# Rounds of 56 instead of 64 token slots per expert in a two-layer mixture-of-experts trunk on one core

## The chip, the core and the metric

The kernel runs on one core of one Trainium2 chip. The metric is the device time of one launch in microseconds (us); less is better. The engines named below are PE (TensorE: matmuls; its weight loads are listed apart as PEld), DVE (VectorE), ACT (ScalarE), POOL (GpSimd) and SP (SyncE, which here only issues DMAs).

## What is computed

Two layers over 256 tokens of 1024 features. Each layer is a mixer (three token mixers, gates, an output projection), a LayerNorm, then a shared expert plus 64 routed experts, then a LayerNorm. The change is in the routed experts:

```python
D_MODEL = 1024; SEQ = 256; DEPTH = 2
N_EXPERTS = 64; TOP_K = 8; N_GROUPS = 8; TOPK_GROUPS = 4; EXPERT_DIM = 256
...
def route(x_flat, router_w, router_bias):
    scores = jax.nn.sigmoid((x_flat @ router_w).astype(jnp.float32))
    choice = scores + router_bias.astype(jnp.float32)
    ...                                   # the best 4 of 8 groups, then the best 8 experts in them
    w = jnp.take_along_axis(scores, idx, axis=-1)
    w = w / jnp.sum(w, axis=-1, keepdims=True) * ROUTED_SCALE
...
    def one_block(args):                  # t: the tokens of a block, g: their gates, ex: its expert
        t, g, ex = args
        h = x_pad[t] @ w_gate_up[ex]
        h = jax.nn.silu(h[:, :EXPERT_DIM]) * h[:, EXPERT_DIM:]
        return (h @ w_down[ex]) * g[:, None]
```

Every token goes to 8 of 64 experts, so an expert gets 32 of the 256 tokens on average. On the inputs of the reference the fullest expert has 47 tokens in layer 0 and 51 in layer 1 (counted from its routing). All weights are float32; those of the experts are 3.1 MB each (1024 x 512 and 256 x 1024), 403 MB over both layers.

## The kernel before

**Slots.** Tokens are grouped by expert into slots. An expert has SLOTS = 64 slots in a round; an expert with more than 64 tokens would need a second round over all experts, and ROUNDS = 4 is the most there can be. `ranks` (L904) computes each token's rank in each of its experts (`slot_of`) and the largest count (`count_f`). `later_rounds` (L933) writes count - 1 as an integer to `count_i` (L936) and three further copies of `slot_of`, less 64, 128 and 192 (L938). `more_rounds` (L364) loads that integer on PE, ACT, DVE and SP and shifts it right by 6: the number of rounds beyond the first.

**Pairs.** Experts are worked two at a time, one pair per `pair_step`: 32 pair steps in a layer and round, 64 in all. The even and the odd pair step of a step number m share one gather for four experts. The pieces on PE, in the order in which PE issues them:

- L1393, "turn": two matmuls of 132 moving columns that turn the one-hot matrix and pick out the gates.
- L1406, up product: for each of 8 slices of 128 features and each of the 2 experts one matmul, 64 token columns held as weights, 512 columns of expert weights moving. Expert 0 writes partitions 0 to 63 of `bank_up`, expert 1 partitions 64 to 127, so the two use different column halves of the array. The trace has two records for each matmul of plain float32.
- L1361, gather (`gather`, L1349): fetches the tokens of four experts as columns. For each of 8 feature slices k, 4 matmuls (2 token halves t, and x split into `xg_hi` and `xg_lo`), each with 128 weight columns of x and 4 x 64 = 256 moving columns of `onehot`. All are float32r, one record each. It comes in quarters q = 0 to 3 of 8 matmuls, placed in the odd pair step only: q0 after the up product, q1 after the transposes, q2 after combine(1), q3 after the down product. Each quarter fills `bank_gather`, which ACT copies to `xe_t` (L696) before the next quarter may start.
- L1378, `combine`: 4 matmuls of 512 columns per half, float32r, for the pair step before.
- L1418: two transposes of `hid`.
- L1432, down product: built like the up product.

ACT applies silu (L707), DVE multiplies gate and up part (L1126), copies `hid_t` (L1129) and `onehot_t` (L1133), and both split the down product into `y_hi` (L713) and `y_lo` (L1140). The one-hot matrix of the next four experts is one DVE comparison of ranks with `iota` (`slots`, L942 to L947), 64 columns for each expert.

**Weights.** SP issues the loads of expert weights (`load_up` L478, `load_down` L482) in a fixed order. Three buffers take the pairs in turn up to pair 25 of a layer, two buffers the last six; a load waits until the up product (L488) or the down product (L492) of the pair before it in that buffer is done. After the last pair of layer 0 SP goes on to the projection weights of layer 1 (L469), whose split on ACT (L594) stands ahead of the last pair's silu.

**Order.** Every engine's program is written out by hand with semaphores; the pair steps are loops of six and of two steps. The lines around the gather:

```python
for c in range(2):
    k = 2 * q + c
    for t in range(TT):
        for part in (xg_hi, xg_lo):
            ins = mm(bank_gather[:, 2 * P * c:2 * P * c + 2 * P], part[:, t, k, :], onehot[:, t, :], ...)
```

Of the kernel before, what the change touches and what calls it, by code (L numbers as in the profile page):

```python
# [26 lines left out]
ALU = mybir.AluOpType  # L27
ACT = mybir.ActivationFunctionType
AX = mybir.AxisListType.X

P = 128
D = 1024
KD = D // P
S = 256
# [5 lines left out]
NE = 64  # L40
# [1 line left out]
FE = 256  # L42
KF = FE // P
SLOTS = 64
ROUNDS = S // SLOTS
GROUPS = 8
TOPK_GROUPS = 4
ROUTED_SCALE = 2.5
# [10 lines left out]
CONST = {}  # L59
CONST_COLS = 0  # L60
for _name, _width in (("ident", P), ("cos", S), ("sin", S), ("rotate", P), ("mask", S), ("iota", SLOTS),
                      ("earlier", GROUPS * GROUPS), ("ones", P), ("ramp", 4 * 16), ("before", P)):
    CONST[_name] = (CONST_COLS, CONST_COLS + _width)
    CONST_COLS += _width

# [71 lines left out]
def build(nc, x, w_in, rel_bias, pool_w, pool_scale, lambda_q1, lambda_k1, lambda_q2, lambda_k2, subln_g,  # L137
# [3 lines left out]
    with ExitStack() as ctx:  # L141
        def sb(name, shape, dt=F32):
            return ctx.enter_context(nc.sbuf_tensor(name, shape, dt))
# [29 lines left out]
        group_r = sb("group_r", [P, TT, GROUPS])  # L173
        wsum = sb("wsum", [P, TT])
        count_f = sb("count_f", [P, 1])
        count_i = sb("count_i", [P, L], I32)


        slot_of = sb("slot_of", [P, TT, ROUNDS * NE])
# [3 lines left out]
        onehot = sb("onehot", [P, TT, 2 * P], F32R)  # L183
# [38 lines left out]
        def view(at, *shape, dt=F32):  # L222
            size = 1
            for n in shape:
                size *= n
            words = size if dt == F32 else size // 2
            v = arena[:, at:at + words]
            if dt != F32:
                v = v.bitcast(dt)
            if len(shape) == 2:  # L230
                v = v.rearrange("p (a b) -> p a b", a=shape[0])
            elif len(shape) == 3:
                v = v.rearrange("p (a b c) -> p a b c", a=shape[0], b=shape[1])
            return v
# [2 lines left out]
        dn_b = view(8192, 2, KF, D)  # L237
        xg_hi, xg_lo = [nc.alloc_sbuf_tensor_at(name, [P, TT, KD, P], F32R, offset=arena_at + 4 * at)
                        for name, at in (("xg_hi", 12288), ("xg_lo", 14336))]
        xe_t = view(16384, KD, 2 * P)  # L240

        y_hi = nc.alloc_sbuf_tensor_at("y_hi", [P, D], F32R, offset=arena_at + 4 * 18432)
        y_lo = nc.alloc_sbuf_tensor_at("y_lo", [P, D], F32R, offset=arena_at + 4 * 19456)
# [26 lines left out]
        bank_gather, bank_even, bank_odd, bank_t = banks[4:8]  # L270
# [46 lines left out]
        count_ready = sem("count_ready")  # L317
# [9 lines left out]
        xe_ready = sem("xe_ready")  # L327
# [36 lines left out]
        def more_rounds(eng, l):  # L364

            eng.wait_ge(count_ready, l + 1)
            most = eng.value_load(count_i[0:1, l:l + 1], min_val=0, max_val=S - 1)
            return eng.snap(most >> 6).with_bounds(min_val=0, max_val=ROUNDS - 1)

        def x_tile(t, j):  # L370

# [213 lines left out]
        def _(act):  # L585
# [11 lines left out]
            for l in range(L):  # L597
                for task in PLAN:
# [19 lines left out]
                    elif kind == "z":  # L618
# [3 lines left out]
                        if name in ("ga", "gb", "gc"):  # L622

                            v = (i - 14) % 4
# [5 lines left out]
                        else:  # L630
                            dst = {"qa": qa_t, "ka": ka_t, "qc": qc_t, "kc": kc_t, "ub": ub_t}[name]
                            ins = nc.scalar.copy(dst[:, 2 * half:2 * half + 2, :], two)
# [60 lines left out]
                def gather_out(m, q):  # L693

                    act.wait_ge(gathered, 4 * m + q + 1)
                    nc.scalar.copy(xe_t[:, 2 * q:2 * q + 2, :],  # L696
                                   bank_gather[:].rearrange("p (c n) -> p c n", c=2)).then_inc(xe_ready, 1)

                def pair_step(n, odd, following=None, last=False):

# [40 lines left out]
        def _(dve):  # L741
            steps = [0]

            def step(ins):

                ins.then_inc(dve_step, 1)
                steps[0] += 1
# [185 lines left out]
            def later_rounds(l):  # L933

                wait_evac(dve, l, ("rank", 0, 0))
                v.tensor_scalar(count_i[:, l:l + 1], count_f[:], -1.0, None, ALU.add).then_inc(count_ready, 1)  # L936
                for r in range(1, ROUNDS):
                    step(v.tensor_scalar(slot_of[:, :, r * NE:(r + 1) * NE], slot_of[:, :, 0:NE], float(-SLOTS * r), None,  # L938
                                         ALU.add))
                settle()  # L940

# [220 lines left out]
        def _(pe):  # L1162
# [33 lines left out]
            for l in range(L):  # L1196
# [153 lines left out]
                def gather(m, q):  # L1350

                    if q == 0:
                        pe.wait_ge(s_ready, m + 1)
                    if q:

                        pe.wait_ge(xe_ready, 4 * m + q)
                    for c in range(2):
                        k = 2 * q + c
                        for t in range(TT):
                            for part in (xg_hi, xg_lo):  # L1360
                                ins = mm(bank_gather[:, 2 * P * c:2 * P * c + 2 * P], part[:, t, k, :], onehot[:, t, :],  # L1361
                                         start=(t == 0 and part is xg_hi), stop=(t == TT - 1 and part is xg_lo))
                    ins.then_inc(gathered, 1)

# [19 lines left out]
                def pair_step(n, m, first, odd, slot, loads, last=False):  # L1384
# [16 lines left out]
                    for k in range(KD):  # L1401
                        if not odd and k % 2 == 0:

                            pe.wait_ge(xe_ready, 4 * m + k // 2 + 1)
                        for e in range(2):
                            ins = mm(bank_up[SLOTS * e:SLOTS * e + SLOTS, :],  # L1406
                                     xe_t[:, k, P * odd + SLOTS * e:P * odd + SLOTS * e + SLOTS],
                                     gu[slot][:, e, k, :], start=(k == 0), stop=(k == KD - 1))
                    ins.then_inc(up_done, 1)
                    if odd and not last:  # L1410
# [64 lines left out]
def _constants():  # L1475
# [5 lines left out]
    def put(name, value):  # L1481
        a, b = CONST[name]
        c[:, a:b] = value
# [17 lines left out]
    mask = np.zeros((P, S), np.float32)  # L1501
    mask[:CHUNK, S - CHUNK:] = NEG
    put("mask", mask)
    put("iota", np.arange(SLOTS, dtype=np.float32)[None, :])
    g = np.arange(GROUPS)
    put("earlier", (g[None, :] < g[:, None]).astype(np.float32).reshape(1, -1))
    put("before", (p[:, None] < p[None, :]).astype(np.float32))
# [31 lines left out]
```

## Time and profile before

| | |
|---|---|
| time, median of 3 runs | 1582.39 us (1580.69 to 1586.14) |
| profiled execution, its own time | 1581.64 us |
| span from first to last instruction in it | 1579.8 us |
| PE busy | 1525.8 us, 97% of the span |
| DVE busy | 565.5 us, 36% |
| ACT busy | 414.4 us, 26% |
| moved by DMA | 495.86 MB, mean 314 GB/s |
| mean granted PE clock | 0.989 of full speed |

1.8 us of the profiled execution's time lie outside the span. An expert stage is the stretch of one layer in which L1406 and L1432 run: about 294 to 780 us and 1079 to 1564 us. The mixer stages lie before each. A PE that is listed as busy is not always computing: the records of matmuls overlap (one of the gather lasts 0.28 us and the next begins 0.12 us after it), so the distance from start to start says more than a record's length.

### The profile page before, as it was taken

How to read it: one execution, taken by the hardware profiler on the slowest of the kernel's cores; microseconds unless marked ns; L12 is line 12 of the kernel's file. 1: busy time of each engine (PE TensorE's matmuls, PEld its weight loads, DVE VectorE, ACT ScalarE, POOL GpSimd, SP SyncE). 2: the span in 40 equal slices, each digit the busy share in tenths (PEclk: the TensorE clock that was granted, in tenths of full speed). 3: DMA queues.
4: the chain of work that ended last, by engine and by line, in shares of the span. 5: the costliest groups of instructions: out<-in, count | busy, mean ns of one | idle time of the engine just before them, and what ended most of it. 6: DMA issues, size and time to landing. Idle time of an engine off the chain costs nothing.

```text
span 1579.8 us, 21900 instructions
## 1 busy us (share of the span) xinstructions
PE 1525.8 (97%) x8898; PEld 948.7 (60%) x8898; DVE 565.5 (36%) x1009; ACT 414.4 (26%) x655; POOL 34.5 (2%) x30
## 2 busy tenths in 40 slices
PE   7999999999999999999789999999999999999996
PEld 7899996444454444445388999864444444544542
DVE  4567735222222222222545577351222222212224
ACT  4545422121111112112235544221111211211111
POOL 0101000000000000000001110000000000000000
PEclk9999999999999999999989999999999999999998
DMA  8543458799999999699733544587999999996991
GB/s 292 175 170 138 153 206 374 288 426 424 415 421 414 405 417 414 244 414 419 282 107 107 187 161 160 210 331 317 426 425 416 419 401 416 419 411 249 415 412 75
DMA packets 79741, 495.86 MB, mean 314 GB/s; under 512 B 6080, under 2 KB 11456, under 8 KB 46656
## 3 DMA queue, kind: packets, MB, share of 16 engines
q1 hardware_dynamic: 77392, 491.31, 76.9%
q10 hardware_dynamic: 2288, 3.67, 0.7%
q8 instruction: 47, 0.77, 0.2%
q14 instruction: 14, 0.11, 0.0%
HBM read 493.92 MB, written 1.05 MB: 313 GB/s over the span
## 4 chain that ended last, share of the span: by engine, by line
PE 94%; DVE 2%; DMA 2%; ACT 1%; issue 1%; SPq 0%; DVEq 0%
PE bank L1406 28%; PE bank L1252 19%; PE bank L1432 14%; PE bank L1361 8%; PE bank L1378 8%; PE bank L1322 4%; PE bank L1209 3%; PE bank L1191 2%; DMA ring_w<-in_w_in 2%; PE bank L1418 1%; PE bank L1393 1%; PE bank L1369 1%; ACT w_hi L594 1%; PE bank L1264 1%; PE bank L1290 1%
## 5 line engine op out<-in xcount | busy, mean ns | idle before, releaser
L1252 PE MATMUL bank<-x_hi,w_hi 128*128 128x256 f32 x688 | 198.4, 288 | 3.5 <-ACT arena L646 1.9
L1252 PE MATMUL bank<-x_lo,w_hi 128*128 128x256 f32 x688 | 195.4, 284 | 0.0
L1252 PE MATMUL bank<-x_hi,w_lo 128*128 128x256 f32 x688 | 195.3, 284 | 0.0
L1126 DVE SCALAR_TENSOR_TENSOR hid<-hid,gate_s,bank 128x256 f32<-128x256 f32 x64 | 30.8, 481 | 399.7 <-ACT hid L707 399.7
L1406 PE MATMUL bank<-arena 128*64 128x512 f32 x768 | 170.1, 595 | 0.0
L1406 PE MATMUL bank<-gu_a,arena 128*64 128x512 f32 x768 | 170.1, 595 | 0.0
L1140 DVE TENSOR_TENSOR y_lo<-bank,y_hi 128x512 fp32r<-128x512 f32 x128 | 88.6, 692 | 225.3 <-ACT y_hi L713 225.3
L777 DVE TENSOR_TENSOR w_lo<-ring_w,w_hi 128x2048 fp32r<-128x2048 f32 x63 | 143.9, 2288 | 66.3 <-ACT w_hi L594 66.2
L1361 PE MATMUL bank<-onehot,xg_hi 128*128 128x256 f32 x512 | 139.9, 306 | 4.0 <-DVE onehot L946 4.0
L713 ACT CAST y_hi<-bank 128x512 fp32r<-128x512 f32 x128 | 74.9, 585 | 246.1 <-PE bank L1432 246.1
L1252 PEld LDWEIGHTS bank<-x_hi,w_hi 128*128 128x128 f32 x688 | 132.7, 193 | 7.5 <-issue 4.0
L707 ACT ACTIVATE hid<-bank 128x256 f32<-128x256 f32 x64 | 24.6, 384 | 426.0 <-PE bank L1406 426.0
L594 ACT CAST w_hi<-ring_w 128x2048 fp32r<-128x2048 f32 x64 | 121.8, 1904 | 45.7 <-PE bank L1322 32.7
L1361 PEld LDWEIGHTS bank<-onehot,xg_hi 128*128 128x128 f32 x512 | 97.2, 190 | 60.3 <-issue 52.8
L1252 PEld LDWEIGHTS bank<-x_lo,w_hi 128*128 128x128 f32 x688 | 132.8, 193 | 0.2
L1252 PEld LDWEIGHTS bank<-x_hi,w_lo 128*128 128x128 f32 x688 | 132.7, 193 | 0.0
L1361 PE MATMUL bank<-onehot,xg_lo 128*128 128x256 f32 x512 | 127.0, 281 | 0.0
L696 ACT COPY arena<-bank 128x512 f32<-128x512 f32 x128 | 75.0, 586 | 152.1 <-PE bank L1361 152.1
L1406 PE MATMUL bank<-ring_w,arena 128*64 128x512 f32 x512 | 113.4, 595 | 0.0
L1406 PEld LDWEIGHTS bank<-arena 128*64 128x64 f32 x768 | 53.0, 137 | 97.7 <-issue 95.9
L1406 PEld LDWEIGHTS bank<-gu_a,arena 128*64 128x64 f32 x768 | 53.0, 137 | 97.7 <-issue 95.9
L1378 PE MATMUL bank<-y_hi,onehot_t 128*128 128x512 f32 x256 | 106.8, 417 | 2.8 <-DVE y_lo L1140 2.8
(186 smaller groups left out, 1996.4 us busy)
## 6 DMA issues: line engine op xcount, KB each, us to landing
gu_a<-in_expert_w_gate_up SPq DMA_DIRECT2D x24, 4096.0 KB, 13.7
arena<-in_expert_w_gate_up SPq DMA_DIRECT2D x24, 4096.0 KB, 14.6
ring_w<-in_expert_w_gate_up SPq DMA_DIRECT2D x32, 2048.0 KB, 10.9
ring_w<-in_w_in SPq DMA_DIRECT2D x25, 2048.0 KB, 8.6
dn_a<-in_expert_w_down SPq DMA_DIRECT2D x24, 2048.0 KB, 12.1
arena<-in_expert_w_down SPq DMA_DIRECT2D x24, 2048.0 KB, 11.2
dn_c<-in_expert_w_down SPq DMA_DIRECT2D x16, 2048.0 KB, 11.7
ring_w<-in_w_out SPq DMA_DIRECT2D x4, 2048.0 KB, 7.9
```

Source lines behind the costliest of these rows:

```text
L594: nc.scalar.copy(chunk_part(w_hi, n), chunk_in(n)).then_inc(w_hi_ready, 1)
L696: nc.scalar.copy(xe_t[:, 2 * q:2 * q + 2, :], bank_gather[:].rearrange("p (c n) -> p c n", c=2)).then_inc(xe_ready, 1)
L713: nc.scalar.copy(y_hi[:, 512 * h:512 * h + 512], (bank_other, bank_up)[h][:]).then_inc(y_hi_ready, 1)
L777: v.tensor_tensor(chunk_part(w_lo, n), chunk_in(n), chunk_part(w_hi, n).bitcast(F32), ALU.subtract).then_inc(w_lo_ready, 1)
L1140: v.tensor_tensor(y_lo[:, part], (bank_other, bank_up)[h][:], y_hi[:, part].bitcast(F32), ALU.subtract).then_inc(y_ready, 1)
L1209: ins = mm(acc[t][h][:], merged[:, k, P * t:P * t + P], slot_of_block(n, KD)[:, k, :], start=(k == 0), stop=(k == KD - 1))
L1252: ins = mm(b[:, S * c:S * c + S], lhs, rhs, start=(k == 0 and a + w == 0), stop=(k == KD - 1 and a == 1))
L1322: ins = mm(b[:, S * c:S * c + S], w_parts[a][:, k, cols], (y_hi_of, y_lo_of)[w][i][:, k, :], start=(k == 0 and a + w == 0), stop=(k == KW ...
L1361: ins = mm(bank_gather[:, 2 * P * c:2 * P * c + 2 * P], part[:, t, k, :], onehot[:, t, :], start=(t == 0 and part is xg_hi), stop=(t == TT ...
L1378: ins = mm(acc[t][half][:], onehot_t[:, P * t:P * t + P], part[:, 512 * half:512 * half + 512], start=False, stop=True, skip_group_check=True)
L1406: ins = mm(bank_up[SLOTS * e:SLOTS * e + SLOTS, :], xe_t[:, k, P * odd + SLOTS * e:P * odd + SLOTS * e + SLOTS], gu[slot][:, e, k, :], sta ...
L1432: ins = mm((bank_other, bank_up)[h][SLOTS * e:SLOTS * e + SLOTS, :], hid_t[:, k, SLOTS * e:SLOTS * e + SLOTS], dn[slot][:, e, k, 512 * h:5 ...
```

## The change

A round covers USED = 56 tokens of each expert; they still stand in 64 slots of the one-hot matrix and of the PSUM partitions. `iota` holds 0 to 55 and then a value no rank has, so the last 8 one-hot columns of an expert are always zero. The gather reads 56 of each 64 one-hot columns (224 moving columns in four runs), writes 224 columns for each k, ACT copies 448 columns instead of 512, and the up product takes 56 token columns as weights and writes 56 of each 64 partitions. The turn, the transposes, the down product and combine keep their shapes. The largest number of rounds becomes 5; how many are needed is counted on DVE, by comparing the largest count with 56, 112, 168 and 224 and adding up, and the engines no longer shift the loaded number. `slot_of` is copied four times instead of three.

```diff
+USED = 56
+ROUNDS = -(-S // USED)
...
+        over = sb("over", [P, ROUNDS - 1])
...
-        xe_t = view(16384, KD, 2 * P)
+        xe_t = view(16384, KD, 4 * USED)
...
-            most = eng.value_load(count_i[0:1, l:l + 1], min_val=0, max_val=S - 1)
-            return eng.snap(most >> 6).with_bounds(min_val=0, max_val=ROUNDS - 1)
+            more = eng.value_load(count_i[0:1, l:l + 1], min_val=0, max_val=ROUNDS - 1)
+            return eng.snap(more).with_bounds(min_val=0, max_val=ROUNDS - 1)
...
-                                   bank_gather[:].rearrange("p (c n) -> p c n", c=2)).then_inc(xe_ready, 1)
+                                   bank_gather[:, 0:8 * USED].rearrange("p (c n) -> p c n", c=2)).then_inc(xe_ready, 1)
...
-                v.tensor_scalar(count_i[:, l:l + 1], count_f[:], -1.0, None, ALU.add).then_inc(count_ready, 1)
+                step(v.tensor_tensor(over[:], count_f[:, 0:1].to_broadcast([P, ROUNDS - 1]), const("rounds"), ALU.is_gt))
+                settle()
+                step(v.tensor_reduce(count_f[:], over[:], AX, ALU.add))
+                settle()
+                v.tensor_scalar(count_i[:, l:l + 1], count_f[:], 0.0, None, ALU.add).then_inc(count_ready, 1)
                 for r in range(1, ROUNDS):
-                    step(v.tensor_scalar(slot_of[:, :, r * NE:(r + 1) * NE], slot_of[:, :, 0:NE], float(-SLOTS * r), None,
+                    step(v.tensor_scalar(slot_of[:, :, r * NE:(r + 1) * NE], slot_of[:, :, 0:NE], float(-USED * r), None,
...
-                                ins = mm(bank_gather[:, 2 * P * c:2 * P * c + 2 * P], part[:, t, k, :], onehot[:, t, :],
+                                picked = onehot[:, t, :].rearrange("p (e s) -> p e s", e=4)[:, :, 0:USED]
+                                ins = mm(bank_gather[:, 4 * USED * c:4 * USED * c + 4 * USED], part[:, t, k, :], picked,
...
-                            ins = mm(bank_up[SLOTS * e:SLOTS * e + SLOTS, :],
-                                     xe_t[:, k, P * odd + SLOTS * e:P * odd + SLOTS * e + SLOTS],
+                            c = USED * (2 * odd + e)
+                            ins = mm(bank_up[SLOTS * e:SLOTS * e + USED, :], xe_t[:, k, c:c + USED],
...
-    put("iota", np.arange(SLOTS, dtype=np.float32)[None, :])
+    put("iota", np.where(np.arange(SLOTS) < USED, np.arange(SLOTS), 2.0 * S)[None, :])
+    put("rounds", USED * np.arange(1.0, ROUNDS)[None, :])
```

## Rows read from the trace of the kernel before

**Rows 1.** The page's chain that ended last: shares of the span by engine.

```profile
PE 94%; DVE 2%; DMA 2%; ACT 1%; issue 1%; SPq 0%; DVEq 0%
```

**Rows 2.** The chain in order, two pair steps: start us, us, what.

```profile
368.01 7.02 PE bank L1406 x32
375.03 1.14 PE bank L1361 x8
...
385.07 7.02 PE bank L1406 x32
```

**Rows 3.** Stretches of two pair steps: length, busy us (instructions) by engine, clock, DMA, GB/s.

```profile
354.54:385.07 30.53, 30.53 (x154) 14.22 (x156) 6.81 (x18) 5.45 (x11) 0.00 (x0) 1.00 1.01 424
...
415.60:446.14 30.54, 30.54 (x155) 14.23 (x156) 6.82 (x18) 5.46 (x11) 0.00 (x0) 1.00 0.99 413
```

**Rows 4.** PE in order of time, one gather quarter: start us, us, engine, line, operation.

```profile
711.05 0.28 PE L1361 MATMUL bank<-onehot,xg_lo 128*128 128x256 f32 x1
...
711.88 0.40 PE L1378 MATMUL bank<-y_hi,onehot_t 128*128 128x512 f32 x1
```

**Rows 5.** PE in order of time, the two turn matmuls of one pair step.

```profile
598.47 0.23 PE L1393 MATMUL bank<-turn_pick,onehot 128*128 128x132 f32 x1
...
598.53 0.27 PE L1393 MATMUL bank<-turn_pick,onehot 128*128 128x132 f32 x1
598.73 0.65 PE L1406 MATMUL bank<-ring_w,arena 128*64 128x512 f32 x2
```

**Rows 6.** Weight loads in order of time: two float32r turns, then the router's float32.

```profile
611.84 0.19 PEld L1393 LDWEIGHTS bank<-turn_pick,onehot 128*128 128x128 f32 x1 [0.81 <-issue]
...
611.95 0.19 PEld L1393 LDWEIGHTS bank<-turn_pick,onehot 128*128 128x128 f32 x1
...
269.63 1.87 PEld L1180 LDWEIGHTS bank<-router_sb,x_t 128*128 128x128 f32 x16
271.42 0.97 PEld L1191 LDWEIGHTS bank<-x_t,ring_w 128*128 128x128 f32 x8
```

**Rows 7.** Groups by line and shape: count, busy us, mean ns, idle us before.

```profile
L1361 PE MATMUL bank<-onehot,xg_hi 128*128 128x256 f32 x512 | 139.9, 306 | 4.0 <-DVE onehot L946 4.0
L1393 PE MATMUL bank<-turn_pick,onehot 128*128 128x132 f32 x128 | 25.7, 283 | 0.0
L1180 PE MATMUL bank<-router_sb,x_t 128*128 128x64 f32 x64 | 7.7, 274 | 1.6 <-ACT x_t L612 1.6
L1393 PEld LDWEIGHTS bank<-turn_pick,onehot 128*128 128x128 f32 x128 | 19.4, 188 | 26.9 <-issue 26.9
L1406 PEld LDWEIGHTS bank<-arena 128*64 128x64 f32 x768 | 53.0, 137 | 97.7 <-issue 95.9
L696 ACT COPY arena<-bank 128x512 f32<-128x512 f32 x128 | 75.0, 586 | 152.1 <-PE bank L1361 152.1
L646 ACT COPY arena<-bank 128x256 f32<-128x256 f32 x12 | 4.1, 381 | 0.0
```

**Rows 8.** Line L478, loads of up weights: time from issue to landing.

```profile
DMA to landing us min/median/max: 7.6/13.4/18.0
```

**Rows 9.** SP in order of time: loads for pairs 6 and 31, then layer 1's weights.

```profile
344.77 0.38 SPq L478 DMA_DIRECT2D gu_a<-in_expert_w_gate_up  x1
...
741.70 0.37 SPq L478 DMA_DIRECT2D arena<-in_expert_w_gate_up  x1
```

**Rows 10.** PE in order of time, last pair step of layer 0.

```profile
764.88 7.09 PE L1406 MATMUL bank<-arena 128*64 128x512 f32 x32
```

**Rows 11.** Who waited for whom: us in total, times, longest us.

```profile
PEld bank L1418 <- DVE hid L1126: 18.2, 34, 2.5
DVE gate_s L1113 <- PE bank L1393: 21.9, 4, 10.5
```

**Rows 12.** All engines in order of time: a quarter that waits; stage entry on DVE.

```profile
378.96 0.19 PEld L1361 LDWEIGHTS bank<-onehot,xg_hi 128*128 128x128 f32 x1 [0.18 <-ACT arena L696]
...
282.83 0.14 DVE L936 TENSOR_SCALAR count_i<-count_f 128x1 int32<-128x1 f32 x1
```

More of the change, by code:

```diff
@@ L44 @@
 SLOTS = 64
-ROUNDS = S // SLOTS
+USED = 56
+ROUNDS = -(-S // USED)
 GROUPS = 8
@@ L61 @@
 for _name, _width in (("ident", P), ("cos", S), ("sin", S), ("rotate", P), ("mask", S), ("iota", SLOTS),
-                      ("earlier", GROUPS * GROUPS), ("ones", P), ("ramp", 4 * 16), ("before", P)):
+                      ("earlier", GROUPS * GROUPS), ("ones", P), ("ramp", 4 * 16), ("rounds", ROUNDS - 1), ("before", P)):
     CONST[_name] = (CONST_COLS, CONST_COLS + _width)
```

## The prediction

> **What bounds the kernel now.** I began with the shares of the chain that ended last: 94% of it is PE, 2% DMA [rows 1]. So what counts is time that PE spends. The chain in order shows where: an up product starts at 368.01 and the next at 385.07, with nothing but PE lines between, and a gather quarter (1.14 us) right behind the up product [rows 2]. The stretches of two pair steps come next: PE is busy for all of the 30.53 us, at full granted clock (2.4 GHz), and DMA is nearly full as well, 413 to 424 GB/s at a share of 0.99 to 1.01 [rows 3]. So two questions decide: how much PE time the edit takes out of those 30.53 us, and whether DMA lets PE have it.
>
> **The gather's 1024 matmuls.** The trace groups them as 512 with xg_hi and as many with xg_lo [rows 7]: 2 layers x 16 gathers x 4 quarters x 8. Inside a quarter seven distances lie between 711.05 and 711.88, 118.6 ns each [rows 4]. 256 columns at 2.4 GHz take 106.7 ns, so 11.9 ns are overhead. With 224 columns the stream is 93.3 ns.
>
> What does a shorter float32r matmul do? The turn is the only one with fewer than 256 moving columns: 132, one record each (128 = 64 pair steps x 2, where the router's float32 has 64 records for 32 matmuls) [rows 7]. Its second matmul starts 60 ns after the first (598.47, 598.53) [rows 5]. 132 columns are 55 ns, so it streams a column per cycle with 5 ns on top: no slower mode for short float32r. Between 5 ns at 132 and 11.9 ns at 256, the overhead at 224 is about 10 ns, and the stream alone would allow 93.3 + 10 = 103 to 104 ns.
>
> But every matmul of the gather has its own 128 weight columns. Two turn loads with nothing ahead of them start 0.11 us apart (611.84, 611.95), though the matmul on them needs only 55 ns. Sixteen loads of the router, whose matmuls have 64 columns, follow each other in 271.42 - 269.63 = 1.79 us, 111.9 ns each [rows 6]; their two passes of 64 columns are 53 ns. So a load of 128 columns sets a floor, and the narrower matmul meets it before its own stream. From these rows the floor is 108 to 112 ns; I take 111, since the sixteen in a row are nearer to the gather's sustained stream than a single pair is.
>
> The Trainium skill ("TensorE: Matmul & The Clock Gate", section "LDWEIGHTS (loading the stationary operand)") gives columns / 1.2 for a load, 106.7 ns for 128; the trace agrees, a few ns above it. Its section "Back-to-back issue gap" gives columns / 2.4 + 2.5 ns for an isolated matmul, by which the edit would give 13.3 ns on each of the 1024, 13.7 us; the trace's 118.6 ns are above that formula's 109 for 256 columns. What its time would be here, by rows, is the second rival.
>
> Saving: 118.6 - 111 = 7.6 ns x 1024 = 7.8 us. The distance to whatever follows a quarter counts, since that too begins with a load. Bounds: 6.8 us at 112, 10.9 us at 108, 15.0 us at 104, and nothing if float32r loads already set the 118.6.
>
> The moving operand is no longer contiguous: four runs of 56 with gaps of 8. No row shows PE reading like that. A price below nothing is excluded, since the columns are the same; above, the nearest price of a break is what starting another matmul costs, 11.9 ns. I take 0: under the floor of 111 up to 7 ns for each matmul are hidden anyway.
>
> **The up product.** Its time is set by 512 moving columns, which stay. Only the weight loads shrink, from 64 to 56 columns. Loads of 64 and of 128 columns last 137 and 188 ns [rows 7], 0.8 ns per column: 6.4 ns, hidden behind the stream in all but the first load of a pair step, which nothing covers after the turn. 64 x 6.4 ns = 0.4 us. That experts 0 and 1 go on running beside each other is assumed: 56 columns of weights in the same halves.
>
> **ACT's copies.** 512 columns take 586 ns, 256 take 381 [rows 7], so 448 take about 535, 51 ns less. Some quarters wait for the copy before them, as the one whose load comes at 378.96 [rows 12], one in each odd pair step of the loops, 30 in all; about 20 ns of each wait show on PE, 0.6 us at most, and as the quarter ahead of it shortens too I count 0.2 us. In the first gather of a layer each quarter hangs more directly on the copy: 6 x 51 ns = 0.3 us, of which the shared down products between them hide some; 0.2 us.
>
> **DVE.** Two more instructions, a fourth copy of slot_of, and two waits on its own results, in each layer. The write of count_i takes 0.14 us [rows 12]; four such pieces with their waits are 0.8 us. They are ahead of DVE's first gate reduction, before which DVE has waited for PE up to 10.5 us [rows 11]: hidden, 0. With that cover gone it would be 1.6 us. SP's wait for count_ready comes that much later, with the down load of pair 2 behind it; loads of that stage have 20 us in hand (below). The shift that PE, ACT, DVE and SP drop is one register operation, 0. The table of constants and slot_of grow, which moves tiles that come after them; 0.
>
> **Does DMA let it through?** Two pair steps need 12.58 MB (four experts). At 424 GB/s [rows 3] that is 29.7 us. PE needs 30.53 now and about 30.3 after (32 x 7.6 ns less), 30.0 with the whole stream saved: both above 29.7. There is also lead. The up load of pair 6 is issued at 344.77 [rows 9]; with the longest landing of 18.0 us [rows 8] it is there at 362.8, and its up product starts at 385.07 [rows 2], 22 us later. With two buffers it is tighter: pair 31, issued 741.70 [rows 9], there by 759.7, used at 764.88 [rows 10], 5 us. Saving 0.12 us on each pair step doesn't use that up in six. In the even steps PE waits for DVE ahead of the transposes, 18.2 us in 34 waits [rows 11]; no gather is there, so nothing of the saving goes into that wait and nothing of the wait goes away.
>
> **Sum.** 7.8 + 0.4 + 0.2 + 0.2 = 8.6 us. The profiled execution took 1581.64 us, which would become 1573.0. The median of the runs is 0.75 us above it, so the forecast is 1582.39 - 8.6 = 1573.8 us, 0.54% faster.
>
> **Rivals.**
> 1. *Nothing comes of it:* the 118.6 ns are already the float32r load, or the gaps of the moving operand cost just what the columns save. For: the load's overhead isn't known in a long stream of float32r. Against: the 0.11 us between the turn's loads [rows 6]. Then 0.8 us are saved: 1581.6.
> 2. *The stream sets the time, not the load:* 104 ns. For: 60 ns at 132 columns [rows 5], where the matmul was handed over before its load can have ended. Against: the sixteen at 111.9 [rows 6]. 15.0 + 0.8: 1566.6.
> 3. *Slower: the gapped operand.* PE starts anew at each of the four runs. If a start costs 11.9 ns as a new matmul's does, a gather matmul takes 93.3 + 4 x 11.9 = 141 ns, 22 ns more than now, x 1024 = 23 us, less 0.8: 1604.7. It decides from about 6.3 ns a run upward (93.3 + 25.3 = 118.6). Against: no row shows any such cost.
> 4. *Slower: the two up products of a pair no longer overlap* with 56 columns of weights. They would take 14 us instead of 7.02 [rows 2] in each of 64 pair steps: some 2030 us. The Trainium skill ("TensorEngine Tiling (Array Packing)", section "When to Use Tiling") allows two column tiles up to 64 weight columns, so by it 56 is no worse; no row shows 56.
> 5. *The change doesn't do what it says:* an expert with over 56 tokens brings a second round of 32 pair steps, 32 x 15.3 = 488 us for a layer. The fullest experts have 47 and 51, so it is all but excluded.
> 6. *DMA takes over:* at 413 GB/s instead of 424, two pair steps need 30.5 us. The lead covers most of it; at worst half of the saving goes, 1578.
>
> **How the numbers follow.** Forecast 0.62, with its own range 1570.7 (108 ns) to 1574.8 (112 ns); rival 1 0.14, rival 2 0.11, rival 3 0.07, rivals 4 and 5 together 0.03, rival 6 0.03. A measurement of this kernel can tell about 0.3%, 4.7 us, from no change; the runs of before alone spread by 5.4 us. Faster by more: forecast and rival 2, 0.73. Within: rivals 1 and 6, 0.17. Slower: rivals 3 to 5, 0.10. The range leaves rivals 3 to 5 out: 1566.0 to 1583.0, rival 1 with a little of the spread above it.
>
> **What the changed profile would show.** Distances of 108 to 112 ns inside a quarter: the floor. 104: rival 2. 118 or more: rival 1 or 3, and then the turn's 60 ns tell that short float32r isn't to blame. The up product's group should last 7.0 us as before, with no more records than before; stretches of two pair steps should be about 30.25 us with 415 GB/s. The copies should take about 535 ns. If up loads are issued as before but land later from step to step, it is rival 6. The prediction is wrong in its core if the distances fall and the stretches don't.

## Result and profile after

The changed kernel takes 1573.16 us, median of 4 runs (1572.75 to 1574.91), against 1582.98 us (1580.69 to 1586.14): a ratio of 0.9941, 95% interval 0.9929 to 0.9953. Measured a second time beside other kernels it gave 0.9946 (0.9932 to 0.9959). The forecast was 1573.8 us and a saving of 8.6 us; the two medians differ by 9.8 us. The profiled execution took 1573.10 us, its span is 1571.3 us: 8.5 us less than before.

The page of the changed kernel, busy us and share of the span by engine, and the shares of its chain (as [rows 1]):

```profile
PE 1516.8 (97%) x8898; PEld 936.6 (60%) x8898; DVE 565.1 (36%) x1015; ACT 407.7 (26%) x655; POOL 34.6 (2%) x30
...
PE 94%; DVE 2%; DMA 2%; ACT 1%; issue 1%; SPq 0%; DVEq 0%
```

PE has lost 9 us and ACT 7 us of busy time; what ends last has not changed. The gather is now L1368, the up product L1414, the down product L1439, combine L1385, the turn L1400, ACT's copy L698. The chain in order over two pair steps (as [rows 2]):

```profile
366.39 7.01 PE bank L1414 x32
373.40 1.08 PE bank L1368 x8
374.48 0.93 PE bank L1385 x4
375.40 0.23 PE bank L1425 x2
375.63 0.89 PE bank L1368 x8
376.52 0.93 PE bank L1385 x4
377.45 0.88 PE bank L1368 x8
378.34 3.58 PE bank L1439 x16
381.92 1.09 PE bank L1368 x8
...
383.19 7.01 PE bank L1414 x32
```

From up product to up product are 16.80 us where [rows 2] has 17.06, and nearly all of it lies in the four gather quarters, the first of which takes 1.08 us where it took 1.14. The up product keeps its 7.0 us. Both pair steps together, as a stretch (columns as in [rows 3]):

```profile
366.25:396.52 30.27, 30.27 (x154) 13.87 (x152) 6.76 (x17) 5.25 (x11) 0.00 (x0) 1.00 1.01 426
```

30.27 us where [rows 3] has 30.53. The 426 GB/s are those of this stretch alone: from 320 to 640 us DMA moved 416 GB/s before and 420 after. PE in order of time, one quarter (as [rows 4]):

```profile
710.28 0.26 PE L1368 MATMUL bank<-onehot,xg_hi 128*128 128x224 f32 x1
710.39 0.27 PE L1368 MATMUL bank<-onehot,xg_lo 128*128 128x224 f32 x1
...
711.06 0.28 PE L1368 MATMUL bank<-onehot,xg_lo 128*128 128x224 f32 x1
```

Six distances lie between 710.39 and 711.06: 111.7 ns each, and these six average 111.7 ns over all 128 quarters too; before it was 118.6. The groups by line (as [rows 7]):

```profile
L1368 PE MATMUL bank<-onehot,xg_hi 128*128 128x224 f32 x512 | 131.2, 295 | 4.0 <-DVE onehot L952 4.0
L1414 PE MATMUL bank<-arena 128*56 128x512 f32 x768 | 169.9, 595 | 0.0
L1414 PEld LDWEIGHTS bank<-arena 128*56 128x56 f32 x768 | 50.4, 130 | 100.1 <-issue 98.3
L698 ACT COPY arena<-bank 128x448 f32<-128x448 f32 x128 | 68.1, 532 | 144.0 <-PE bank L1368 144.0
```

The up product has the same number of records, 595 ns each; its loads take 130 ns instead of 137; the copies 532 instead of 586.

**Where the 8.5 us come from.** I laid PE's instructions of both traces side by side, one by one (8898 in each), and read at five marks how far the changed kernel was ahead. The last column is the second trace of the changed kernel, against the same trace of before:

| stretch | gain, first trace | gain, second trace |
|---|---|---|
| start to the first full projection | -0.8 us | -1.2 us |
| entry of layer 0's expert stage, to its first up product | +1.9 | +1.9 |
| 31 pair-step distances of layer 0 | +3.9 | +3.8 |
| from there to the projections of layer 1 | -2.3 | 0.0 |
| entry of layer 1's stage | +1.9 | +0.2 |
| 31 pair-step distances of layer 1 | +3.9 | +3.9 |
| all | +8.5 | +8.6 |

Only the two stages repeat: the 31 distances of a layer (their sum is called the stage sum below) add up to 471.15 us before and 467.2 to 467.3 us after, 7.8 us in all (7.7 by the second trace). The other lines mostly follow the granted clock. Stretches of the kernel before and then of the changed one, at the entry of the stage (columns as in [rows 3]; the third number from the end is the clock, 0.60 in the first row):

```profile
282.00:284.00 2.00, 2.00 (x5) 0.91 (x5) 1.28 (x9) 0.58 (x1) 0.00 (x0) 0.60 1.01 434
284.00:286.00 2.00, 2.00 (x7) 1.21 (x6) 0.00 (x0) 0.00 (x0) 0.00 (x0) 0.55 0.81 344
```

```profile
282.00:284.00 2.00, 2.00 (x11) 1.39 (x12) 1.79 (x10) 0.53 (x1) 0.00 (x0) 1.00 0.85 360
284.00:286.00 2.00, 2.00 (x12) 1.42 (x11) 0.69 (x5) 0.38 (x1) 0.00 (x0) 1.00 1.03 442
770.00:776.00 6.00, 5.75 (x20) 2.30 (x22) 3.48 (x5) 0.59 (x1) 0.00 (x0) 0.72 0.99 346
```

Before, PE ran at about half clock (1.2 GHz) after its 2 us of idleness for the routing, and the two rows count 12 matmuls in those 4 us; after, it had 2.4 GHz and they count 23. The changed kernel had its half clock at the handover (770 to 776 us): PE had waited 2.2 us for the last pair's silu, which ACT does behind its split of layer 1's weights, and the last down product took 5.3 us instead of 3.6.

### The profile page after: what moved, and what is told of

It is laid out like the page before. It is cut to its first block, busy times and chain, and to the rows that moved or that the text cites. A ratio compares the mean times of both kernels' runs of the same rounds, so it can differ in the third digit from the quotient of the medians.

```text
span 1571.3 us, 21899 instructions
## 1 busy us (share of the span) xinstructions
PE 1516.8 (97%) x8898; PEld 936.6 (60%) x8898; DVE 565.1 (36%) x1015; ACT 407.7 (26%) x655; POOL 34.6 (2%) x30
## 4 chain that ended last, share of the span: by engine, by line
PE 94%; DVE 2%; DMA 2%; ACT 1%; issue 1%; SPq 0%; DVEq 0%
PE bank L1414 28%; PE bank L1258 19%; PE bank L1439 14%; PE bank L1368 8%; PE bank L1385 8%; PE bank L1328 4%; PE bank L1215 3%; DMA ring_w<-in_w_in 2%; PE bank L1197 2%; PE bank L1425 1%; PE bank L1400 1%; PE bank L1376 1%; ACT w_hi L596 1%; PE bank L1270 1%; PE bank L1296 1%
## 5 line engine op out<-in xcount | busy, mean ns | idle before, releaser
L1414 PE MATMUL bank<-arena 128*56 128x512 f32 x768 | 169.9, 595 | 0.0
L1414 PE MATMUL bank<-gu_a,arena 128*56 128x512 f32 x768 | 169.9, 595 | 0.0
L1368 PE MATMUL bank<-onehot,xg_hi 128*128 128x224 f32 x512 | 131.2, 295 | 4.0 <-DVE onehot L952 4.0
L1368 PEld LDWEIGHTS bank<-onehot,xg_hi 128*128 128x128 f32 x512 | 97.9, 191 | 58.2 <-issue 52.5
L1368 PE MATMUL bank<-onehot,xg_lo 128*128 128x224 f32 x512 | 121.0, 275 | 0.0
L1414 PE MATMUL bank<-ring_w,arena 128*56 128x512 f32 x512 | 113.3, 595 | 0.0
L1385 PE MATMUL bank<-y_hi,onehot_t 128*128 128x512 f32 x256 | 107.6, 420 | 2.8 <-DVE y_lo L1146 2.8
L1414 PEld LDWEIGHTS bank<-arena 128*56 128x56 f32 x768 | 50.4, 130 | 100.1 <-issue 98.3
L1414 PEld LDWEIGHTS bank<-gu_a,arena 128*56 128x56 f32 x768 | 50.3, 130 | 100.1 <-issue 98.3
L698 ACT COPY arena<-bank 128x448 f32<-128x448 f32 x128 | 68.1, 532 | 144.0 <-PE bank L1368 144.0
```

The source lines that it names most:

```text
L698: nc.scalar.copy(xe_t[:, 2 * q:2 * q + 2, :], bank_gather[:, 0:8 * USED].rearrange("p (c n) -> p c n", c=2)).then_inc(xe_ready, 1)
L1368: ins = mm(bank_gather[:, 4 * USED * c:4 * USED * c + 4 * USED], part[:, t, k, :], picked, start=(t == 0 and part is xg_hi), stop=(t == TT ...
L1385: ins = mm(acc[t][half][:], onehot_t[:, P * t:P * t + P], part[:, 512 * half:512 * half + 512], start=False, stop=True, skip_group_check=True)
L1414: ins = mm(bank_up[SLOTS * e:SLOTS * e + USED, :], xe_t[:, k, c:c + USED], gu[slot][:, e, k, :], start=(k == 0), stop=(k == KD - 1))
```

## Experiments

The kernels for which no ratio is given (four widths, contiguous operand, full copies, no low part) ran once each; they are read by their traces.

**The changed kernel again, the kernel before again.** Do the other lines of the table belong to the change?

> The changed kernel as it is, once more, for its ratio and for where the half-clock stretches lie. In the two traces so far the 31 pair-step distances of a layer's expert stage add up to 471.2 us before and 467.2 us after, 7.8 us for both layers; the rest of the 8.5 us between the spans is the sum of a gain of 1.9 us at each stage's entry, a loss of 0.8 us at the start and one of 2.3 us between the layers. Theory: the 7.8 us are the change's own and return in every execution, and the other four mostly follow half-clock stretches of PE that lie elsewhere in each execution. Then the ratio is 0.993 to 0.996, the sums are again 467.2 us, and at least one of the other four has another size. Rival: entry and tail are the change's own too; then all four return within 0.3 us.

> The kernel before, once more, as a run of its own. It says what the trace of one execution can't: how far the start, the entries and the handover between the layers differ from execution to execution, and whether a kernel compared with itself gives 1.000. Theory: the ratio is 1.000 within 0.0010; the stage sums are 471.15 us again within 0.1 us; the half-clock stretches of PE stand at other places than in the first trace of this kernel. Rival: the stretches stand at the same places, so that they belong to the kernel.

The changed kernel gave 0.9946 and stage sums of 467.30 us in both layers; the handover was 0.0 instead of -2.3 us and the entry of layer 1 +0.2 instead of +1.9. The kernel before, as a run of its own, gave 1.0000 (0.9991 to 1.0009) and sums of 471.14 us. Its trace had no half clock at the entry of layer 0 and some at the handover, the other way round than its first trace:

```profile
282.00:284.00 2.00, 2.00 (x11) 1.35 (x11) 1.83 (x12) 0.59 (x1) 0.00 (x0) 1.00 0.92 393
```

So the 7.7 to 7.8 us are the change's, and the half-clock stretches fall differently in each execution of either kernel; each cost 1.7 to 1.9 us. This second trace of before also gives what the first could not, an entry of layer 0 at full clock on both sides: there the changed kernel gains 0.25 us in either of its traces. In layer 1, at half clock on both sides, its second trace gains 0.2 us.

**Fewer slots still.** Is 112 ns the weight load or the stream of moving columns?

```diff
-USED = 56
+USED = 52
```

> 52 slots instead of 56 (the fullest expert has 51 tokens): 208 moving columns in the gather, 52 weight columns in the up product, 416 columns in the copies. Load-floor theory: the 128 weight columns of each gather matmul set the distance, so it stays at 111 to 112 ns though the stream is 6.7 ns shorter; the time is within 1 us of the changed kernel's, a ratio of about 0.994. Stream theory (the 7 ns of the change were the shorter stream with more overhead): another 6 to 7 ns for each of 1024, 6 to 7 us, a ratio of about 0.990, distances of 105 ns.

Ratio 0.9946 (0.9932 to 0.9959), the same as the changed kernel beside it; stage sums 467.02 us, 0.2 to 0.3 us less. PE in order of time:

```profile
712.15 0.27 PE L1368 MATMUL bank<-onehot,xg_lo 128*128 128x208 f32 x1
...
712.82 0.27 PE L1368 MATMUL bank<-onehot,xg_lo 128*128 128x208 f32 x1
```

0.67 us for six distances again, 111.7 ns (112.2 over all quarters), though 208 columns are 6.7 ns less than 224. The stream theory falls.

**A width for each quarter.**

```diff
-    picked = onehot[:, t, :].rearrange("p (e s) -> p e s", e=4)[:, :, 0:USED]
-    ins = mm(bank_gather[:, 4 * USED * c:4 * USED * c + 4 * USED], part[:, t, k, :], picked,
+    wide = (56, 48, 40, 32)[q]
+    picked = onehot[:, t, :].rearrange("p (e s) -> p e s", e=4)[:, :, 0:wide]
+    ins = mm(bank_gather[:, 4 * USED * c:4 * USED * c + 4 * wide], part[:, t, k, :], picked,
```

> The changed kernel with another width of the moving operand in each quarter of the gather: 224, 192, 160 and 128 columns (56, 48, 40 and 32 of each expert's slots); the slots left out are not gathered in three of four quarters, so part of the features of the later tokens is stale. The weights stay at 128 columns for each matmul. Load-floor theory: distances of 110 to 112 ns in all four quarters. Stream theory: 112, 98, 84 and 70 ns. Mixed: a fall between 224 and 192 and then a floor, at 105 to 108 ns, would say that 224 still lay on the stream.

PE in order of time, a quarter with 160 and one with 128 columns:

```profile
710.20 0.27 PE L1369 MATMUL bank<-onehot,xg_lo 128*128 128x160 f32 x1
...
710.87 0.27 PE L1369 MATMUL bank<-onehot,xg_lo 128*128 128x160 f32 x1
...
714.82 0.28 PE L1369 MATMUL bank<-onehot,xg_lo 128*128 128x128 f32 x1
...
715.49 0.27 PE L1369 MATMUL bank<-onehot,xg_lo 128*128 128x128 f32 x1
```

Again 0.67 us for six in each: 111.7 ns from 224 down to 128 columns. The first distance of a quarter, behind another kind of matmul, does shrink: from 206 to 164 ns in the quarter of 128 columns and from 103 to 75 ns in that of 160, about what 96 and 64 columns stream in (40 and 27 ns). Part of it is lost again: the two turn matmuls behind the quarter of 128 columns stand about 116 ns apart, where the changed kernel has 69. So the 60 ns of [rows 5] are not a pace that such matmuls keep. Stage sums are 466.8 us, 0.45 us less for 43% fewer columns in one quarter, 29% and 14% in the others. The Trainium skill ("TensorE: Matmul & The Clock Gate", "LDWEIGHTS (loading the stationary operand)") has columns / 1.2 for a load, 106.7 ns; the trace's floor is 5 ns above it. Its section "Back-to-back issue gap" also states a sustained 81 ns for 128 columns; here the distances inside a quarter of 128 columns stayed at 111.7 ns, in float32r.

The type matters. The changed kernel's trace has five bf16 matmuls in a row, with 128 weight columns each and 64 moving ones:

```profile
279.50 0.19 PE L1339 MATMUL bank<-sel_b,before_b 128*128 128x64 bf16 x1
279.53 0.19 PE L1340 MATMUL bank<-sel_b,ones_b 128*128 128x64 bf16 x1
```

They start 28 to 30 ns apart, so the floor of 112 ns is one of float32 and float32r. No run changed the number of weight columns in the gather: that the floor is the load, and not something else that such a matmul pays whatever its moving columns, rests on [rows 6] and on where the loads lie in the gather. With 256 and 448 columns the next load begins 3 ns after a matmul has begun (median), with 224 columns 9 ns after, and in the kernel with four widths 35 ns after (up to 54), while the distances stay at 112 ns: the narrower the matmul, the later its successor's load.

**The other side of the floor.** If each load costs 112 ns, fewer and wider matmuls must win.

```diff
-                    for c in range(2):
+                    for c in range(1):
...
-    picked = onehot[:, t, :].rearrange("p (e s) -> p e s", e=4)[:, :, 0:USED]
-    ins = mm(bank_gather[:, 4 * USED * c:4 * USED * c + 4 * USED], part[:, t, k, :], picked,
+    picked = onehot[:, t, 0:4 * USED].unsqueeze(1).to_broadcast([P, 2, 4 * USED])
+    ins = mm(bank_gather[:, 0:8 * USED].rearrange("p (c n) -> p c n", c=2), part[:, t, k, :], picked,
```

> The work of a gather for eight experts instead of four: each quarter has 4 matmuls of 448 moving columns (the 224 twice) instead of 8 of 224; half of the feature slices are left out and the columns stand twice, so the output has other tokens' features. Total moving columns are the same, weight loads are halved. Load-floor theory: a matmul of 448 columns streams longer than its load lasts, so the distance is 187 ns and 12 to 17 ns on top, 199 to 204 ns, and a quarter takes 4 x 202 = 808 ns instead of 8 x 112 = 896: 88 ns x 128 = 11 us faster than the changed kernel, a ratio of about 0.987, if DMA lets it: two pair steps would need 29.93 us and 12.58 MB / 425 = 29.6 us. Rival: what costs is the columns, at 0.5 ns each, not the load; then the distance is 224 ns and the time that of the changed kernel.

```profile
703.12 0.36 PE L1368 MATMUL bank<-onehot,xg_lo 128*128 128x448 f32 x1
703.32 0.36 PE L1368 MATMUL bank<-onehot,xg_hi 128*128 128x448 f32 x1
703.52 0.37 PE L1368 MATMUL bank<-onehot,xg_lo 128*128 128x448 f32 x1
703.73 0.40 PE L1385 MATMUL bank<-y_hi,onehot_t 128*128 128x512 f32 x1
```

Distances of 205 ns, just above the 199 to 204 expected, for the columns of two matmuls that took 223. The ratio is 0.9883 (0.9868 to 0.9898), 1563.93 us, stage sums 463.0 us. A quarter became 65 to 68 ns shorter than in the changed kernel, not 88, so the stages gained 8.5 us where the expectation's 88 ns make 10.6 for their 120 quarters; 12 of the missing 20 ns are the four distances of 205 instead of 202. This kernel leaves half of the feature slices out; it gives the price of a gather for eight experts, not such a gather.

**The gapped operand.** Rival 3's cause, taken away:

```diff
-    picked = onehot[:, t, :].rearrange("p (e s) -> p e s", e=4)[:, :, 0:USED]
+    picked = onehot[:, t, 0:4 * USED]
```

> The gather's moving operand is the first 224 columns of the one-hot matrix in one run, instead of four runs of 56 with gaps of 8; the tokens gathered are those of other slots, the work is the same. Theory: PE reads the gapped operand at no price, so the distances stay at 111.7 ns. Rival: part of the 111.7 ns is the three breaks, and without them the distance falls to 104 ns (the stream with 10 ns on top), 7 us in all.

Mean distance 112.1 ns, stage sums 467.2 us, as with gaps. The breaks could still cost up to about 8 ns a matmul, hidden under the floor (111.7 less the 103 to 104 ns forecast for the stream); more than that they don't.

**The up product with 64 weight columns.**

```diff
-    c = USED * (2 * odd + e)
-    ins = mm(bank_up[SLOTS * e:SLOTS * e + USED, :], xe_t[:, k, c:c + USED],
+    c = min(USED * (2 * odd + e), 4 * USED - SLOTS)
+    ins = mm(bank_up[SLOTS * e:SLOTS * e + SLOTS, :], xe_t[:, k, c:c + SLOTS],
```

> One part undone: the up product holds 64 weight columns again, the gather stays at 224. For the last expert of four the 64 columns begin 8 too early, so that expert's tokens stand in shifted rows; the amount of work is exactly that of 64. Theory: the first load of each up product lies open behind the turn, so the distance from its first to its second pair of matmuls goes back from 474 to 480 ns and nothing else moves: 0.4 us in 64 steps, stage sums of 467.4 us. Rival: the up product's width doesn't matter at all, and 474 is the gather's doing: then it stays at 474 and the sums at 467.2.

The distance from the first pair of up matmuls to the second went from 474 back to 480 ns, the stage sums to 467.5 us. The ratio, 0.9959 (0.9943 to 0.9975), can't tell so little.

**The copies.**

```diff
-        xe_t = view(16384, KD, 4 * USED)
+        xe_t = view(16384, KD, 2 * P)
...
-    bank_gather[:, 0:8 * USED].rearrange("p (c n) -> p c n", c=2)
+    bank_gather[:].rearrange("p (c n) -> p c n", c=2)
...
-    mm(bank_gather[:, 4 * USED * c:4 * USED * c + 4 * USED], part[:, t, k, :], picked,
+    mm(bank_gather[:, 2 * P * c:2 * P * c + 4 * USED], part[:, t, k, :], picked,
```

> The changed kernel, but ACT copies the whole bank of 512 columns again (the gather's 224 columns stand at 0 and 256); 64 stale columns are copied and never read. Theory: copies take 586 ns instead of 532, and only the quarter that waits for the copy before it feels that: the distance from the up product of the odd pair step to the next grows by 0.03 to 0.05 us from 16.80, so the stage sums are 0.4 to 0.8 us longer than 467.2. Rival: nothing waits for the copies within a stage: 467.2 again.

Groups of ACT and PE's waits in this kernel:

```profile
L698 ACT COPY arena<-bank 128x512 f32<-128x512 f32 x128 | 75.0, 586 | 140.9 <-PE bank L1368 140.9
...
PEld bank L1368 <- ACT arena L698: 5.3, 30, 0.2
```

The 30 waits of quarters for the copy before them, which the changed kernel has no longer, are back. The quarter behind combine(1), the one that waits, takes 991 ns instead of 976. Stage sums are 467.46 us against 467.23: 0.23 us a layer, less than the 0.4 to 0.8 expected.

**Counting on VectorE, and the layout alone.** First the changed kernel with 64 slots:

```diff
-USED = 56
-ROUNDS = -(-S // USED)
+USED = 64
+ROUNDS = S // USED
```

> One part alone: rounds are counted on VectorE as in the change, but a round covers 64 tokens as before (256 moving columns, 64 weight columns, full copies). Theory: VectorE's added instructions are hidden behind its wait for PE's first turn, so the ratio is 1.000 within its interval and the pair-step distances of a stage add up to 471.2 us. Rival: the longer VectorE chain at the entry of each expert stage reaches PE: 0.5 to 0.8 us for each layer, a ratio of 1.001, seen as a later first up product behind the last shared down product.

Here the expectation missed: 1.0012 (1.0003 to 1.0021), 1583.79 us, 2 us more, and stage sums of 471.53 us. Yet the added work is small; DVE in order of time at the entry of layer 0:

```profile
284.48 0.15 DVE L938 TENSOR_TENSOR over<-count_f,cst 128x3 f32<-128x3 f32 x1
284.67 0.16 DVE L940 TENSOR_REDUCE count_f<-over 128x1 f32<-128x3 f32 x1
284.86 0.15 DVE L942 TENSOR_SCALAR count_i<-count_f 128x1 int32<-128x1 f32 x1
```

That is 0.4 us more than the single instruction of before, once a layer; but the stage grew in every odd pair step, which holds the gather, from 17.06 to 17.08 us on average, and the distances in the gather from 118.6 to 119.2 ns. The even steps stayed the same. Work done once a layer can't do that; tiles at other addresses might. So the kernel before with the new columns and tile, unused:

```diff
-("ramp", 4 * 16), ("before", P)):
+("ramp", 4 * 16), ("rounds", ROUNDS - 1), ("before", P)):
...
         count_f = sb("count_f", [P, 1])
+        over = sb("over", [P, ROUNDS - 1])
```

> The kernel that only counts rounds on VectorE took 0.12% longer than before (2 us), with 0.38 us more in each stage sum (471.53 against 471.15) and 1.6 us more before the first projection, where its first weights landed 9.9 us after their issue instead of 8.2. This kernel has its layout alone: three more columns in the table of constants (rows of 5900 bytes instead of 5888) and the small tile for the comparisons, neither used; rounds are counted the old way. Layout theory: ratio 1.001 again, stage sums 471.5, first landing near 9.9 us. Counting theory: the added VectorE work made it, so here the ratio is 1.000, the sums are 471.15 and the landing 8.2 us. Chance theory: the landing is 8.2 here and would be in another execution of the other, and the ratio is 1.000.

The layout theory held for the ratio, 1.0012 (1.0003 to 1.0021), and for the sums, 471.53 and 471.55 us; the first landing was 8.2 us, so the 9.9 us of the other trace do not belong to the layout. PE in order of time:

```profile
711.55 0.28 PE L1362 MATMUL bank<-onehot,xg_hi 128*128 128x256 f32 x1
...
712.26 0.40 PE L1379 MATMUL bank<-y_hi,onehot_t 128*128 128x512 f32 x1
```

Six distances in 0.71 us, about 118 to 119 ns; their mean over all quarters is 119.0. The counting costs nothing that can be seen; where the tiles lie costs 0.8 us in the stages. About 1 us more in the median has no place in the traces, and it is less than one half-clock stretch costs. The change's own layout is again another: 16 bytes more in a row of constants, a tile of 16 bytes, and a fourth copy of `slot_of`.

**The change with its new pieces padded.**

```diff
-("rounds", ROUNDS - 1)
+("rounds", 16)
...
-        over = sb("over", [P, ROUNDS - 1])
+        over_wide = sb("over", [P, 16])
+        over = over_wide[:, 0:ROUNDS - 1]
...
```

> The changed kernel with its two new pieces of layout padded: 16 columns for the thresholds in the table of constants instead of 4 (rows of 5952 bytes instead of 5904) and a tile of 16 words for the comparisons; everything else is the change. Three columns and a small tile alone cost 2 us of time and 0.38 us in each stage with gathers of 256 columns. Address theory: the change pays such a price as well and the padding takes part of it back: a ratio of 0.993, with distances in the gather or stage sums below 467.2 us. Hidden theory: within the stages the load floor of 112 ns covers it; the sums stay at 467.2 us, the distances at 111.7 ns, and the ratio at 0.9945 within its interval.

0.9953 (0.9941 to 0.9964), distances 111.8 ns, stage sums of 467.43 and 467.42 us, 0.1 to 0.2 us longer than in the two traces of the changed kernel: nothing came back. The address theory is not borne out for this padding.

**Does DMA take over?**

```diff
-                            for part in (xg_hi, xg_lo):
+                            for part in (xg_hi,):
...
-    start=(t == 0 and part is xg_hi), stop=(t == TT - 1 and part is xg_lo))
+    start=(t == 0), stop=(t == TT - 1))
```

> The gather leaves out the low part of x: half of its matmuls are gone, 32 of each two pair steps become 16. It asks where DMA takes over. PE theory: each two pair steps lose 16 x 112 ns = 1.8 us, from 30.28 to 28.5 us, 52 us in all, and DMA delivers at 442 GB/s. DMA theory: weights arrive at no more than 425 GB/s, so two pair steps take at least 12.58 MB / 425 = 29.6 us once the lead of 20 us is used up; with a deficit of 1.1 us for each two steps the lead lasts for about the whole stage of 3 buffers but the last six steps with two buffers wait. Then the stage sums are between 440 and 455 us, the up product begins to wait for its weights late in the stage, and landings take longer than 18 us.

A stretch, the landings of the up weights, the chain at the handover, PE's last transposes of layer 0, and the clock around them:

```profile
574.00:604.00 30.00, 30.00 (x146) 12.51 (x142) 7.20 (x18) 5.83 (x11) 0.00 (x0) 1.00 1.01 426
...
DMA to landing us min/median/max: 7.6/19.2/28.5
...
720.06 24.89 DMA ring_w<-in_w_in
...
747.79 0.71 PE L1425 MATMUL bank<-cst,hid 128*128 128x128 f32 x2 [6.84 <-DVE hid L1132]
...
744.00:754.00 10.00, 6.21 (x16) 2.75 (x18) 5.64 (x5) 2.31 (x3) 0.00 (x0) 0.50 0.61 213
```

The stage sums were 440.47 us: PE kept its own pace of 28.5 us for two pair steps to the end. DMA stood at 425 to 427 GB/s and fell behind, landings grew from 18 to 28.5 us, and the lead of the up weights (from landing to use) shrank from 20.6 us at pair 2 to 6.6 at pair 25 and 3.5 at pair 31, by 1.0 us in each two steps. It was never gone, so the up product never waited; what was owed was paid at the handover. Layer 1's first weights took 24.9 us instead of 20.7, PE waited 6.8 us instead of 2.2 for the silu behind their split, and the distance from the last up product of layer 0 to the first of layer 1 grew from 314.4 to 318.5 us. Some of this growth is clock: half clock lasted from 744 to 754 us here. The expectation had the ceiling right and put the payment in the wrong place.

## Why the prediction was right, and where only the sum was

- **Gather.** Forecast 7.6 ns for each of 1024, 7.8 us. The distance fell from 118.6 to 111.7, 6.9 ns, and the quarters of the stages became shorter by 55 to 79 ns, averaged by place in the step, where 61 had been forecast. That this total came out is partly luck: the forecast took a quarter for eight equal distances. Six of them gave 35 to 42 ns together. The first, 133 to 223 ns long before depending on what precedes it, gave 16 to 30, and the last 3 to 7. In the stages 120 of the quarters lie, 7.3 us forecast; 7.8 us were measured there together with the up product and the copies, 7.9 forecast. The floor of 111 ns that I took from the router's loads [rows 6] is within 1 ns of what the kernels with 52 slots and with four widths measured, 111.7 to 112.2.
- **Short float32r.** Read from the 60 ns of [rows 5], and right in its result: no slower mode down to 128 columns. The 60 ns themselves are found between the turn's matmuls only in the odd steps of the loops, right behind a gather quarter; in the even ones they are some 160 ns apart. They say that a stream this short is possible, not that matmuls follow each other at it, and the 10 ns of overhead worked out from them for 224 columns was never tested, since the floor lies over it.
- **Up product.** Forecast 0.4 us, measured 6 ns in each of 64 steps, 0.4 us. The two experts still run side by side at 56 columns (rival 4).
- **Copies.** Forecast 0.2 us in the loops with 0.6 as the end; the kernel with full copies measured 0.46. Mis-sized: the quarter behind combine(1) gained about 15 ns more than a shorter gather alone gives, 30 times. Some 0.3 us of what quarters, copies and up product gained was lost elsewhere in the odd steps, most of it between the turn's two matmuls, 69 ns apart instead of 63.
- **Entry of a stage.** Forecast 0.2 us for the copies and 0.5 us for the first gathers' own share, 0.7 us over both layers. Where both traces had the same clock it was 0.25 us in layer 0 and 0.2 us in layer 1, less than 0.5 us in all: the gathers' share, with nothing left for the copies. Most of the 1.9 us of the other entries is clock, which the sum did not have, and in the first trace they are nearly offset by -0.8 at the start and -2.3 at the handover. That the span fell by 8.5 us is thus 7.8 us of the stages, some 0.45 us of the two entries by the comparison at equal clock, and a rest in which half-clock stretches nearly cancel: that it met 8.6 us so closely is luck.
- **DVE, 0; tables and slot_of, 0.** The first held. The second was wrong for gathers of 256 columns: in the median the new layout alone cost 2 us, of which 0.8 us are seen in the stages. Against a kernel with such a layout and 64 slots the stage sums fell by 4.2 to 4.3 us a layer, 8.5 us; against before by 7.8. Whether the change still pays the rest of that price is open, since no run had its gathers in the old layout.
- **DMA.** Forecast: lets it through, at 415 GB/s. It did, at 420 GB/s from 320 to 640 us, and without the low part it let a further 1.8 us in each two steps pass, on the lead it had.
- **Rivals 1 and 2** would have saved 0.8 and 15.8 us; the four widths exclude the second, the measured 111.7 ns the first. Rival 3 fell with the contiguous operand, rival 5 with the 64 pair steps in the trace.

## What to carry to other kernels

Before narrowing a matmul's moving operand, look for the distance at which loads of that many weight columns and of that type follow each other: here 112 ns for 128 in float32 and float32r. So below about 240 columns (256 less 6.9 ns at 0.417 ns a column, an estimate from the two distances) next to nothing more is gained: 52 slots took 0.2 to 0.3 us less a layer than 56, the four widths 0.45. Below that floor the next step is fewer loads with wider operands (205 ns for 448 columns against 223 for two of 224). Compare a stage by the sum of its step distances rather than by the span: the sums of one kernel agree to 0.1 us between executions whose entries and handovers differ by up to 1.9 us with the clock.

## What the runs showed of the hardware

- Float32r with 128 weight columns, distance from start to start at 2.4 GHz: 112 ns for 128, 160, 192, 208 and 224 moving columns, 118.6 for 256, 205 for 448.
- Bf16 with 128 weight and 64 moving columns: 28 to 30 ns, five in a row.
- Half-clock stretches (1.2 GHz) that follow PE's idle time at a stage's entry or a handover come in some executions and not in others of the same kernel, and cost 1.7 to 1.9 us each.
- A few bytes of layout (12 bytes more per row of a constant table and a 12-byte tile) moved the mean distance of float32r matmuls with 256 columns from 118.6 to 119.0 or 119.2 ns, the stage sums by 0.4 us each and the kernel by 0.12% (interval 0.03% to 0.21%); what in the address does it was not found.
- With DMA at its ceiling of 425 GB/s, a deficit of 1.0 us in each two steps was carried through a whole stage, with three weight buffers to pair 25 and two behind it.
